# Odd contraction tiles of the dense products streamed from the last column to the first

## The reference, cut to what matters

```python
def swiglu(h, w1, w3, w2):
    return (jax.nn.silu(h @ w1) * (h @ w3)) @ w2
...
    for layer in range(DEPTH):
        ...
        if layer % 2 == 0:
            fc, st = gla_ssd_features(hc, zero_states_gla_ssd(bsz), *pa)
            fx, _ = gla_ssd_features(hx, st, *pa)
            w_o = a_w_out[j]
        else:
            fc, st = mlstm_features(hc, zero_states_mlstm(bsz), *pb)
            fx, _ = mlstm_features(to_colmajor(hx), st, *pb)
            fx = from_colmajor(fx)
            w_o = b_w_down[j]
        x = x + mx[2] * (fx @ w_o)
        x = x + mx[5] * swiglu(modulate(rmsnorm(x, norm_ffn[layer]), mx[3], mx[4]),
                               ffn_w1[layer], ffn_w3[layer], ffn_w2[layer])
```

## Time and profile before

| | |
|---|---|
| median of 3 runs | 2491.22 us (2489.59 to 2496.49) |
| the profiled execution | 2485.69 us, of which the span of the instructions is 2483.8 us |
| mean granted TensorE clock | 0.979 |
| PE busy | 2341.4 us, 94% of the span |
| weight loads busy | 1866.0 us, 75% |
| DVE busy | 1451.8 us, 58% |
| POOL busy | 1070.4 us, 43% |
| ACT busy | 623.0 us, 25% |

### The profile page before, as it was taken

How to read it: one execution, slowest core, us unless ns; L and a number is a source line. 1 busy time by engine, 2 the same in 40 slices (tenths; PEclk the granted TensorE clock), 3 DMA queues, 4 the chain that set the end, 5 groups by cost and what they waited for, 6 DMA issues and landing times.

```text
span 2483.8 us, 33401 instructions
## 1 busy us (share of the span) xinstructions
PE 2341.4 (94%) x12131; PEld 1866.0 (75%) x12131; DVE 1451.8 (58%) x2482; ACT 623.0 (25%) x1018; POOL 1070.4 (43%) x815
## 2 busy tenths in 40 slices
PE   5999999999878999999999989999999989999998
PEld 3878888888534788888888878876555557888886
DVE  4584778784586368877876646545467655111113
ACT  3202354343595131000000133223212202200002
POOL 2343343344553425463554344344211035666664
PEclk8999999999998999999999999999999999999999
DMA  7753342344540344444444213344333112333332
GB/s 274 216 174 100 100 128 85 113 161 138 186 133 24 85 76 111 119 119 125 112 119 119 80 48 121 128 155 133 100 98 110 47 43 84 93 94 101 93 93 85
DMA packets 390134, 280.98 MB, mean 113 GB/s; under 512 B 31106, under 2 KB 355228, under 8 KB 390012
## 3 DMA queue, kind: packets, MB, share of 16 engines
q1 hardware_dynamic: 334220, 203.61, 28.3%
q10 hardware_dynamic: 55792, 75.71, 9.0%
HBM read 237.21 MB, written 42.07 MB: 112 GB/s over the span
## 4 chain that ended last, share of the span: by engine, by line
PE 60%; DVE 6%; issue 1%; ACT 1%; DMA 0%; POOL 0%; DVEq 0%; ACTq 0%; SPq 0%; POOLq 0%
PE PS L895 44%; PE PS L1394 3%; PE PS L1565 3%; PE PS L1406 3%; PE PS L1517 2%; PE PS L836 1%; PE PS L1485 1%; PE PS L904 1%; DVE xcr L2349 1%; PE PS L830 0%; PE PS L1349 0%; PE PS L1466 0%; DVE rdiag L2278 0%; DVE hh L2920 0%; DVE hh L2918 0%
## 5 line engine op out<-in xcount | busy, mean ns | idle before, releaser
L715 POOL TENSOR_TENSOR w_hi<-w_raw,ones 128x128 fp32r<-128x128 f32 x244 | 153.2, 628 | 1246.1 <-DMA w_raw<-in_ffn_w 432.8
L895 PE MATMUL PS<-act_hi,w_hi 128*128 128x512 f32 (+1 forms) x1824 | 656.7, 360 | 21.9 <-DVE act_lo L2308 11.3
L895 PE MATMUL PS<-act_lo,w_hi 128*128 128x512 f32 (+1 forms) x1824 | 639.8, 351 | 0.0
L895 PE MATMUL PS<-act_hi,w_lo 128*128 128x512 f32 (+1 forms) x1824 | 636.3, 349 | 0.0
L718 POOL TENSOR_TENSOR w_lo<-w_raw,w_hi 128x1024 fp32r<-128x1024 f32 (+1 forms) x244 | 594.6, 2437 | 20.4
L895 PEld LDWEIGHTS PS<-act_hi,w_hi 128*128 128x128 f32 x1824 | 348.1, 191 | 76.8 <-issue 17.7
L895 PEld LDWEIGHTS PS<-act_lo,w_hi 128*128 128x128 f32 x1824 | 347.7, 191 | 46.1 <-issue 1.2
L895 PEld LDWEIGHTS PS<-act_hi,w_lo 128*128 128x128 f32 x1824 | 346.0, 190 | 47.5
L2251 DVE SCALAR_TENSOR_TENSOR mf_acc<-mf_ring,cs,mf_acc 128x128 f32<-128x128 f32 x784 | 277.8, 428 | 2.0
L716 POOL TENSOR_SCALAR w_hi<-w_raw 128x896 fp32r<-128x896 f32 (+1 forms) x244 | 245.7, 1007 | 0.0
L2531 DVE SCALAR_TENSOR_TENSOR xT<-PS,modv,xT 128x512 f32<-128x512 f32 (+1 forms) x120 | 74.9, 657 | 233.1 <-PE PS L895 204.0
(11 more groups left out here) (352 smaller groups left out, 3569.8 us busy)
## 6 DMA issues: line engine op xcount, KB each, us to landing
w_raw<-in_ffn_w SPq DMA_DIRECT2D x120, 512.0 KB, 3.9
mf_ring<-in_w_mod SPq DMA_DIRECT2D x56, 512.0 KB, 4.0
w_raw<-in_a_w_in SPq DMA_DIRECT2D x44, 512.0 KB, 4.1
proj<-stage ACTq DMA_DIRECT2D x44, 384.0 KB, 3.9
w_raw<-in_b_w_up SPq DMA_DIRECT2D x32, 512.0 KB, 4.6
m_ring<-in_w_mod SPq DMA_DIRECT2D x12, 1024.0 KB, 8.6
rows<-g_d SPq DMA_DIRECT2D x16, 768.0 KB
m_raw<-in_w_mod SPq DMA_DIRECT2D x4, 2048.0 KB, 12.4
```

The source lines that it names most:

```text
L715: pool.tensor_tensor(w_hi[:, s, 0], w_raw[:, s, 0], ones[:], ALU.mult)
L895: last = pe.matmul(to[:, c0:c1], w[:, s, k, :], x[:, k, c0:c1], start=k == 0 and w is w_hi and x is hi, stop=k == kt - 1 and w is w_lo)
```

## The change

For odd k both the moving operand and the PSUM destination are given as views with a step of -1: the product reads the activations' columns from the last to the first and writes the bank's columns from the last to the first. For even k nothing changes. Each column of the output gets the same terms in the same order. The number of instructions, their order, their shapes and the weight loads stay as they are.

```diff
+            def columns(x, k):
+
+                return x[:, ::-1] if k % 2 else x
+
             def tile_products(s, k, kt, hi, lo, n, at=None):
                 to = slot(s if at is None else at)
                 for c0, c1 in ((0, 512), (512, 768))[:1 if n == LAT else 2]:
                     for w, x in ((w_hi, hi), (w_hi, lo), (w_lo, hi)):
-                        last = pe.matmul(to[:, c0:c1], w[:, s, k, :], x[:, k, c0:c1],
+                        last = pe.matmul(columns(to[:, c0:c1], k), w[:, s, k, :], columns(x[:, k, c0:c1], k),
                                          start=k == 0 and w is w_hi and x is hi, stop=k == kt - 1 and w is w_lo)
                 return last
```

## The result

The changed kernel takes 2501.99 us (median of 6 runs, 2496.67 to 2503.66); the kernel before took 2490.55 us beside it (median of 6, 2489.14 to 2496.49). The ratio is 1.0038 with a 95% interval of 1.0023 to 1.0054, so the change costs some 9.5 us where no change was forecast. The half rate did not come.

What follows compares the result with a forecast made beforehand. PE was taken as the bound, busy 94% of the span. Price of a reversed column, turn and time between products were each 0, so the forecast was the unchanged median, 2491 us, with a range of 2468 to 3070 us.

Steps and rivals of the forecast that it cites:

- half rate: Rival: TensorE takes descending columns at half the rate on read or write side; plus 558 us, near 3049 us, chance 0.27.
- PE is the bound, and a nanosecond on its products goes to the end: Whole kernel: PE, busy 94% of the span, passes changes in dense products' cost to the end one for one.
- Which products are touched, 3528 of 7056: Odd k: 1368 pairs (512 and 256) and 792 products of 512 are reversed, together 662 us or 27% of the span.
- Price of a reversed column, 0: Reversed products: direction costs nothing; bounded by 200 ns per 512, 292 ns per pair, and -56 us in all as floor.
- the time between products: Gap between products' starts in reversed stretches: may shift either way by 2.6%, 17 us on 662; taken as 0.
- the two readings of the rule: PSUM access: by the cacheline a descending run is contiguous and free; by the word it costs the half rate's sum.
- The turn, 0 with a bound of 68 us: With n = LAT, 401 changes of k restart at the column just written and might wait for PSUM's sum; taken as 0.
- The second rival: A dearer turn or less lucky time between products: about 2508 us either, 2524 both; 2499 to 2559 us given 0.14.

Runs made afterwards that it cites:

- the kernel with n = LAT alone: Odd k reversed only with n = LAT, against the kernel before: 2500.73 us, ratio 1.0030 (1.0016 to 1.0045).

## Why the prediction failed

Point by point, by its own steps.

*PE is the bound, and a nanosecond on its products goes to the end.* Right: at equal clock the kernel with n = LAT alone is 7.1 us slower for 7.0 us of steps and the one with every k reversed 16.5 for 15.4, with standard errors of 1.0 and 1.4. Three readings beside it were off without changing the argument: one slice has PE at seven tenths, the clock stands at nine or more in 38 slices and not 39, and the DVE's 128 columns take 0.40 us and not 0.3.

*Which products are touched, 3528 of 7056.* Right as a count, and not enough as a list of who pays: forward products pay as well, with act and n = LAT 16 ns for each k that follows a backward one.

*Price of a reversed column, 0.* Right as to the rate, on both sides: no kind of backward product steps by more than 240 ns on average, and 429 was the upper bound. The few ns that a backward read does cost belong to the item on the time between products. Of the two readings of the rule of the Trainium skill in "PSUM — Partial Sum Buffer", Specifications, the trace agrees with the one by the cacheline: with the write alone reversed, a descending run over neighbouring columns, the piece took 332.68 us against 332.73. Whether any other pattern slows matmuls no run here shows. The rival of the half rate, to which I gave 0.27 and 558 us, is out.

*The turn, 0 with a bound of 68 us.* This step failed. There is a turn that costs, and I looked for it in the wrong place: at the sum in PSUM, where the bank is the same. It is in the reading of SBUF. It takes 16 + 3 ns for two changes of direction of act with n = LAT, 176 times, 3.3 us, and not in the first product alone: the three forward ones after a turn step by 237.5, 231.8 and 226.7 ns. With n = T, where I excluded a turn, there is one as well and it gives time back: a forward k of act takes 1035.5 ns after a backward one and 1049.3 after a forward one.

*The time between products, 0 because neither side is favoured.* This step failed too. One side was favoured: act with n = LAT stood at the cheapest distance of those tried, 680 ns, and the three others cost 700 or more, as does a backward read at either distance tried. The row that said so was there, 227 against 233 ns for act and hid; I took it for a spread around a middle, but it was the floor beside the usual value. Reversing takes act from the floor (20 ns x 176 = 3.5 us) and leaves hid, which was not on it. Why a k read backward costs 700 ns is open: the read starts at the last of 512 columns, 4 bytes short of a multiple of 128 from where the forward one starts, and it runs through the addresses the other way, and no run tells these two apart. The sum by these two terms is 3.5 + 3.3 = 6.8 us with act and n = LAT; the other three kinds together give -0.3 us.

The second rival named both mechanisms with 2508 us for either and 2524 for both. It had the sign and, in "the act stretches lie at the cheap end now", the reason; its size was too large, because it priced 2.6% over all 662 us, when only the 120 us of act with n = LAT had a cheap place to lose. It should have been the forecast.

What remains between 6.5 us of steps and 9.5 us of time may lie in the clock of the few runs compared, which is not shown; the interval of the ratio, 5.7 to 13.4 us, holds both.

## What to carry to other kernels

In a PE-bound kernel with a weight load ahead of each product, the distance of starts is a finer measure than the kernel's time. Compare it between stretches of the same shape before you cost a change in how operands are read: where one stretch already steps at a floor and another doesn't, the first has little to gain and something to lose. Where the moving operand and the weights start is a free parameter; here it moved a k by up to 23 ns of 700. Try it for each shape, since the cheapest place differed between n = LAT and n = T, and expect little in all: putting hid at the cheap distance took 3.3 us off its piece and was too small for twelve runs of the whole kernel to show.

## What was not expected of the hardware

TensorE's reading of the moving operand depends on how it lies to the weight load that runs beside it. For 512 float32r columns with 128 x 128 weights the distance of starts was 226.7 ns at a distance of 0 modulo 128 bytes and 233.3 to 234.3 at 32, 64 and 96; moving a buffer by 64 bytes turned the one into the other, both ways. Whether the pattern repeats every 128 bytes or every 256 was not tried. The Trainium skill, "TensorE: Matmul & The Clock Gate", Part 2, says that the two reads have ports of their own and that loading the next weights doesn't take read bandwidth from the running matmul; a cost of 20 ns per three products that comes and goes with their relative address, all else equal, is not what that leads one to expect. What in the two reads meets was not tried. A backward read costs 233.3 at both distances tried, 0 and 64, the write's direction costs nothing, and the first products after a change of the read's direction step by up to 240 ns.
